# Splitting the first loads of a trunk kernel between two issuing engines

## What is computed

```python
h     = rmsnorm(x, norm_mix);  mem_n = rmsnorm(mem, norm_mem)
z     = h @ w_in               # columns: q, k, v (8 heads), u (pooling), qx (4 heads), 3 gates
sb    = stick_breaking_attention(q, k, v)          # causal, 128-query blocks
pl    = multiscale_pool(u, w_pool, pool_scale)     # trailing means of 2/4/8/16 frames
xa    = memory_cross_attention(qx, mem_n, w_kv_mem)
x     = x + (sig(g0)*(sb @ w_up_sb) + sig(g1)*(pl @ w_up_pool) + sig(g2)*(xa @ w_up_x)) @ w_out
h     = rmsnorm(x, norm_ffn)
x     = x + hier_moe(h)        # top-1 group of 4, then top-2 of its 4 experts, SwiGLU, 1024->512->1024
out   = rmsnorm(x, norm_final)
# rmsnorm(x, g) = x * rsqrt(mean(x*x) + eps) * g
```

## Time and profile before

| | |
|---|---|
| median of three executions | 726.44 us (725.73 to 727.07) |
| the profiled execution | 727.5 us, its span 725.7 us |
| TensorE matmul busy | 703.0 us, 97% of the span |
| VectorE, ScalarE, GpSimd busy | 518.5, 402.8, 132.9 us |
| bytes moved by DMA | 159.15 MB, mean 219 GB/s |
| mean granted TensorE clock | 0.994 |

### The profile page before, as it was taken

The page is one execution under the profiler, slowest core; times in us unless marked ns, Lnnn a source line. Parts: engine busy times, 40 slices in busy tenths (PEclk is TensorE's granted clock), DMA queues, the critical chain, the costliest instruction groups (busy, mean ns, idle before and its releaser), DMA issues.

```text
span 725.7 us, 10014 instructions
## 1 busy us (share of the span) xinstructions
PE 703.0 (97%) x3581; PEld 588.2 (81%) x3581; DVE 518.5 (71%) x550; ACT 402.8 (55%) x411; POOL 132.9 (18%) x144
## 2 busy tenths in 40 slices
PE   7999999999999999999999999999999999999982
PEld 6898888888888888888889868888888888888871
DVE  4788776898527062350735778999999999999975
ACT  6716665676523132221413537777777777777742
POOL 5320000000000000000000133433333333333132
PEclk9999999999999999999999999999999999999997
DMA  9685320000242332332584359999999999999486
GB/s 317 169 264 188 116 86 31 30 1 16 77 141 61 113 101 92 112 101 76 214 333 159 146 213 414 414 377 380 388 383 385 381 393 383 387 392 385 206 165 182
DMA packets 67297, 159.15 MB, mean 219 GB/s; under 512 B 6274, under 2 KB 37116, under 8 KB 63172
## 3 DMA queue, kind: packets, MB, share of 16 engines
q1 hardware_dynamic: 59088, 137.38, 51.7%
q0 software_dynamic: 8128, 21.37, 9.3%
q10 hardware_dynamic: 52, 0.01, 0.0%
HBM read 150.64 MB, written 15.73 MB: 229 GB/s over the span
## 4 chain that ended last, share of the span: by engine, by line
PE 86%; DMA 5%; DVE 4%; ACT 3%; issue 1%; POOL 1%; POOLq 0%; SPq 0%; DVEq 0%; ACTq 0%
PE ps L520 25%; PE ps L522 24%; PE ps L521 24%; DMA x<-y_rows 3%; PE ps L1640 2%; PE ps L1698 2%; DMA xn<-in_x 1%; PE ps L1590 1%; PE ps L1562 1%; PE ps L1420 1%; PE ps L1666 1%; DVE soft L1961 1%; PE ps L1382 1%; ACT ring_hi L482 1%; PE ps L1384 1%
## 5 line engine op out<-in xcount | busy, mean ns | idle before, releaser
L488 DVE TENSOR_TENSOR ring_lo<-raw_a,ring_hi 128x2048 fp32r<-128x2048 f32 (+2 forms) x58 | 115.5, 1995 | 97.0 <-ACT ring_hi L482 97.0
L488 DVE TENSOR_TENSOR ring_lo<-raw,ring_hi 128x2048 fp32r<-128x2048 f32 x71 | 162.2, 2291 | 8.6 <-ACT ring_hi L482 7.3
L482 ACT ACTIVATE ring_hi<-raw 128x2048 fp32r<-128x2048 f32 x71 | 136.3, 1922 | 20.3 <-PE ps L522 20.3
L482 ACT ACTIVATE ring_hi<-raw_a 128x2048 fp32r<-128x2048 f32 (+2 forms) x58 | 97.4, 1680 | 33.6 <-PE ps L522 30.6
L520 PE MATMUL ps<-hT_hi,ring_hi 128*128 128x512 f32 x288 | 113.6, 394 | 1.6 <-DVE hT_lo L1817 1.0
L522 PE MATMUL ps<-hT_hi,ring_lo 128*128 128x512 f32 x288 | 112.4, 390 | 0.0
L521 PE MATMUL ps<-hT_lo,ring_hi 128*128 128x512 f32 x288 | 112.4, 390 | 0.0
L520 PE MATMUL ps<-ring_hi,xT_hi 128*128 128x512 f32 x240 | 95.4, 398 | 0.1
L522 PE MATMUL ps<-ring_hi,xT_lo 128*128 128x512 f32 x240 | 94.1, 392 | 0.0
L521 PE MATMUL ps<-ring_lo,xT_hi 128*128 128x512 f32 x240 | 93.8, 391 | 0.0
L520 PEld LDWEIGHTS ps<-hT_hi,ring_hi 128*128 128x128 f32 x288 | 54.1, 188 | 13.2 <-issue 1.2
(11 more groups left out here) (371 smaller groups left out, 1257.9 us busy)
## 6 DMA issues: line engine op xcount, KB each, us to landing
raw<-in_w_down SPq DMA_DIRECT2D x25, 1024.0 KB
raw<-in_w_gate SPq DMA_DIRECT2D x47, 512.0 KB
raw<-in_w_up SPq DMA_DIRECT2D x47, 512.0 KB
raw_a<-in_w_in SPq DMA_DIRECT2D x15, 1024.0 KB
raw_a<-in_w_gate SPq DMA_DIRECT2D x17, 512.0 KB
raw_a<-in_w_up SPq DMA_DIRECT2D x17, 512.0 KB
raw_a<-in_w_down SPq DMA_DIRECT2D x7, 1024.0 KB
raw_a<-in_w_in SPq DMA_DIRECT2D x10, 512.0 KB, 8.4
```

The costliest lines, as they stand in the source:

```text
L482: act.activation(ring_hi[:, c[0] % SPLIT, 0:width], buf[:, 0:width], ACT.Copy).then_inc(hi_ready, 1)
L488: dve.tensor_tensor(ring_lo[:, s, 0:width], buf[:, 0:width], ring_hi[:, s, 0:width].bitcast(F32), ALU.subtract).then_inc(lo_ready, 1)
```

## The change

SyncE issues blocks 0 and 1 of x, then the four norm vectors, then goes on with the qx weights as before. ScalarE issues blocks 2 and 3 of x in the place where it issued the norm vectors. Semaphores, counts, destinations and all waits stay as they are.

```diff
-            for t in range(TB):
+            for t in (0, 1):
                 sp.dma_start(xn[:, t, :], x[0, t * P:(t + 1) * P, :]).then_inc(x_in[t], 16)
+            sp.dma_start(gain_rows[0:KD, :], norm_mix[0].rearrange("(k p) -> k p", p=P)).then_inc(gain_in, 16)
+            sp.dma_start(gain_rows[KD:2 * KD, :], norm_mem[0].rearrange("(k p) -> k p", p=P)).then_inc(gain_in, 16)
+            sp.dma_start(gain_rows[2 * KD:2 * KD + 2, :], pool_scale[0].rearrange("(k p) -> k p", p=P)).then_inc(gain_in, 16)
+            sp.dma_start(gain_rows[2 * KD + 2:3 * KD + 2, :], norm_ffn[0].rearrange("(k p) -> k p", p=P)).then_inc(gain_in, 16)
             sp.dma_start(raw_a[:, 0, 0:1024].rearrange("p (k n) -> p k n", k=4),
                          rows(win, 0, 4, COL_QX, COL_QX + 256)).then_inc(qx_half, 16)
...
-            act.dma_start(gain_rows[0:KD, :], norm_mix[0].rearrange("(k p) -> k p", p=P)).then_inc(gain_in, 16)
-            act.dma_start(gain_rows[KD:2 * KD, :], norm_mem[0].rearrange("(k p) -> k p", p=P)).then_inc(gain_in, 16)
-            act.dma_start(gain_rows[2 * KD:2 * KD + 2, :], pool_scale[0].rearrange("(k p) -> k p", p=P)).then_inc(gain_in, 16)
-            act.dma_start(gain_rows[2 * KD + 2:3 * KD + 2, :], norm_ffn[0].rearrange("(k p) -> k p", p=P)).then_inc(gain_in, 16)
+            for t in (2, 3):
+                act.dma_start(xn[:, t, :], x[0, t * P:(t + 1) * P, :]).then_inc(x_in[t], 16)
             act.preload_act_table_set("natural_log_exp_and_others")
```

## The result

The change made the kernel slower: 730.64 us in the median of five executions (728.99 to 731.38) against 727.07 for the kernel before (725.73 to 728.62), a ratio of 1.0044 with a 95% interval of 1.0023 to 1.0065. In a second measurement, with 12 executions against 29, the ratio was 1.0044 again (1.0029 to 1.0060). That is +3.2 us. The forecast was +1.9, on a baseline of 726.44, with a range that ended at 730.2.

What follows compares the result with a forecast made beforehand. TensorE was taken to bound the middle, so a later first projection moves the end equally. Late block 1 gave +1.90 us, all other terms 0: 726.44 + 1.90 = 728.3 us, range 725.8 to 730.2.

Steps and rivals of the forecast that it cites:

- The order of the blocks: Load of x: block 1 lands third or fourth, blocks 2 and 3 wait behind it; last square 1.25 to 2.54 us later, taken as 1.90.
- the 0.9 us hole: Load of x, 4.5 to 6.5 us: bandwidth dip missing 0.36 MB against 393 GB/s, or 0.9 us of transfer.
- The dip doesn't come back: Rival, load of x: two queues fill the dip; 726.1 with block 1 third, 727.4 with it fourth; chance 0.25.
- 5.21 us: From the start of the last square (9.59) to the first projection (14.80): taken as unedited by the change.
- the norm vectors: Behind block 1 on SyncE's queue: land at about 9 to 10 us instead of 7.05, costed at 0.
- a fall of the clock: Rival, TensorE's clock: slower case, half of it left out above the range's end of 730.2; chance 0.10.
- The deadline of 11.1 us: TensorE ahead of the transposes: gains may land as late as 11.1 us at no cost.

Runs made afterwards that it cites:

- Experiment 3: Changed kernel with blocks of x dealt out otherwise: 0 and 2 on SyncE, 1 and 3 on ScalarE; ratio 1.0026, +1.9 us against the kernel before.
- Experiment 4: Kernel before with blocks 2 and 3 of x moved to ScalarE, behind the four norm vectors, which stay there; ratio 1.0036.
- experiment 7: Kernel before, DMAs untouched: 4 instead of 12 warm-up matmuls, ratio 1.0001; or five filler matmuls in TensorE's gaps, ratio 1.0004.
- experiment 8: Changed kernel with 22 warm-up matmuls and filler behind the transposes of blocks 0, 1, 2, ratio 1.0039; beside it the changed kernel again, 1.0044.
- The pairs: Changed kernel with blocks 0 and 2 on SyncE, 1 and 3 on ScalarE, 1.0026; also with 22 instead of 12 warm-up matmuls, 1.0027.
- experiment 10: Kernel before, unchanged, profiled three times more; first projection at 14.36, 13.82 and 13.72 us.
- experiment 2: Kernel before with only the four norm vectors moved, to SyncE behind the four blocks of x; ratio 1.0022, +1.6 us.
- experiment 9: Changed kernel with blocks 0 and 2 on SyncE, 1 and 3 on ScalarE, norm vectors on GpSimd's queue, 14 warm-up matmuls; ratio 1.0022.

## Why the prediction was wrong

**What held.** The place was right: only the first 15 us changed, what moved the first projection moved the end (1.67 us in the two profiles, 1.5 in their spans), and the second queue gave no room (393 GB/s from 3 to 8.5 us, what one queue moved from 2.5 to 3 us). Block 1 was in for its square at 8.51, between the 8.30 and 9.56 forecast, and blocks 2 and 3 waited behind it. Experiment 3 shows the mechanism: with the same queues and the blocks dealt out in the order of use, the last square is back at 9.41.

**The order of the blocks: right in size, by luck.** This term was forecast at 1.90 us (1.25 to 2.54) and measured 1.99: the last square starts at 10.91 in the mean of the two traces of the changed kernel, and at 8.92 in the mean of the six whose loads are those of the kernel before. Two errors cancel in it. The forecast put the last square of the changed kernel at 9.59 + 1.90 = 11.49, 0.6 us too late. And the 9.59 that it counted from lies 0.7 us above the mean, since that profile had the 0.9 us hole, which I read as a property of the kernel and asked only whether it would come back after the change. In its depth it was a property of that execution. The rival "The dip doesn't come back" was nearer to the load as it ran, without a hole from 3 us on, but it counted its gain from a median of runs as if they all had the hole.

**The step that failed: all that stands behind this term was put at 0.** From the last square to the projection the sum carried over 5.21 us, "none of which the change edits"; the norm vectors were costed at 0; a fall of the clock was given a chance of 0.10. From the last square to the projection the six traces take 5.28 us in the mean, the two of the changed kernel 5.48 and 6.10, so that the projection is 2.5 us later (16.70 against 14.20). The rest of the measured 3.2, 0.7 us, lies behind the projection and is not tied to a row.

- *GpSimd, 0.2 us.* Its operation on `ms` takes 0.65 instead of 0.38 us in the chain of the changed kernel. The squares follow each other closely there, and the operation runs beside VectorE's scaling of the block before: it ends at 12.88, the scaling at 12.83. In the kernel before with early squares the way is longer too (5.63 and 5.30 us).
- *The gains and the clock, 0 to 0.6 us.* The deadline of 11.1 us was worked out with transposes of 1.09 us. The gains came at 9.03 and met it. But TensorE had waited for them, and the clock fell in both traces of the changed kernel. In the first it read 1.00 again from 12.5 us on, before the transposes of block 3 (1.10 us), and the cost is nil; in the second only from about 15.5 us on, and the cost is 0.6 us.

The chance of 0.10 for the clock was thus for the right event, with too little weight. No run shows the price of a fall with which the range was carried up to 730.2; in the two traces of the changed kernel the fall cost 0 and 0.6 us, ahead of the projection, and neither shows a projection at a lower clock. Experiment 4 does, at 0.50, and takes 712.7 us behind the start of the projection, some 1.9 us more than the traces without a fall. Nor does a granted clock of 1.00 always stand for the same pace: it reads 1.00 for the eight warm-up matmuls of experiment 7, which take 2.08 us, 0.26 each, and for six of the same matmuls as filler in experiment 8, which take 0.83 us, 0.14 each.

**The baseline.** The forecast added 1.90 to 726.44, a median of three executions, with a spread of 0.7 us. In the measurement of the result the kernel before took 727.07, in the later ones 727.62, 728.10 and 728.19, with executions from 725.38 to 731.09. Of the 2.3 us between 728.3 and 730.64, 0.6 come from there.

**What stays open.** The 0.7 us behind the projection are less than the interval. Executions of the changed kernel with a mean clock of 0.983 to 0.986 must have had falls elsewhere than the two traces show; an early fall and one at about 400 us together would give such a mean (an estimate: the former takes 0.005 off 0.994, the latter 0.002 in the trace of experiment 8 and 0.007 in the one of experiment 7), but whether the change makes the latter more frequent isn't settled. The pairs lose 1.9 us, of which a projection 0.7 to 0.8 us later explains less than half; at an equal clock they lose 0.9, so most of the rest goes with a lower clock, and whether two queues cost something beside is not tested. What made the hole in the first profile isn't known either. A weak one stands at the same place in most traces that load x on one queue: from 5.0 to 5.5 us 74 GB/s in the first, 358, 397 and 328 in experiment 10, 300 and 295 in experiment 7, 303 in experiment 2. The changed kernel has 410 and 385 there.

## What to carry to other kernels

A second issuing engine didn't widen a load that already filled the DMA engines (a DMA share of 0.98); it mixed the transfers, so what was used first came later. Deal transfers over queues in the order of use, and count what stands on the other queue at the same time. Before a term of a few tenths of a percent is sized on one profiled execution, ask which of its waits could be that execution's alone: a hole in a transfer for which the program gives no reason is a candidate. Take the baseline from more than three executions, and compare executions at an equal clock only where the clock fell in the same places.

## What the runs showed of the hardware

Two queues shared the DMA engines evenly. In the changed kernel block 0 on SyncE and block 2 on ScalarE were issued at 0.79 and 0.78 us and landed 4.9 and 5.1 us later; alone, block 0 had landed 3.2 us after its issue, at 4.0. Had one of the two been served whole ahead of the other, it would have come at about 4.0 us (an estimate from block 0 alone). Neither did, nor in experiment 3, where the two that were issued together landed 4.8 and 5.0 us after it. So they were mixed. How much the engines took from one queue at a time isn't shown; the profile counts 288 packets for the 1.05 MB on ScalarE's queue, and the two blocks on it have 256 rows.

TensorE's granted clock fell to 0.50 after 2.58 us without work in the changed kernel and stayed at 1.00 through 1.62 us in the kernel before. The length of the gap alone doesn't decide: the clock stayed at 1.00 through 2.02 us in experiment 3 and through 3.30 us in experiment 7 (where the transposes behind the gap took 0.22 us each all the same), and fell to 0.50 about a microsecond after a gap of 1.81 us in experiment 9. At about 400 us it fell in six of sixteen traces while TensorE was busy (0.53 from 396 to 400 us in experiment 7).

The norm vectors came no sooner on a third queue: on GpSimd's the four of them, 13 KB, were issued from 2.15 us on and used at 9.13, behind two blocks of x on SyncE's at 9.08 (experiment 3).
